# Inverses of 32x32 blocks kept beside the rest of the 64x64 matrix, one product per level, in a transformer block on one Trainium2 core

## The reference

```python
p = rmsnorm(x) @ w_in                    # RWKV-7 part, gated-DeltaNet part, two gates
y_a = (groupnorm(rwkv7_recurrence(...)) + bonus) * out_gate      # 32 heads of 64
# gated DeltaNet, 16 heads of 128, in chunks of 64 frames:
lower = jnp.where(strict, einsum(kb, k) * decay, 0.0)            # 64x64, strictly lower
tmat = triangular_solve(eye + lower, eye)                        # its unit-triangular inverse
u = tmat @ vb; wk = tmat @ (kb * exp(gc))                        # then a scan over 4 chunks
x = x + rmsnorm((sigmoid(gA) * y_a + sigmoid(gB) * y_b) @ w_out)
x = x + rmsnorm((silu(xn @ w_gate) * (xn @ w_up)) @ w_down)      # xn = rmsnorm(x)
```

## Time and profile before

| what | value |
|---|---|
| median of 3 runs | 2117.68 us (2117.16 to 2118.33) |
| profiled execution, its own time | 2115.33 us |
| its span, first to last instruction | 2113.6 us |
| TensorE busy | 2079.8 us, 98% |
| VectorE busy | 1423.1 us, 67% |
| ScalarE busy | 1095.8 us, 52% |
| GpSimd busy | 160.7 us, 8% |
| mean granted TensorE clock | 0.997 of full speed |

### The profile page before, as it was taken

How to read it: one execution, slowest core, us unless ns; L and a number is a source line. 1 busy time by engine, 2 the same in 40 slices (tenths; PEclk the granted TensorE clock), 3 DMA queues, 4 the chain that set the end, 5 groups by cost and what they waited for, 6 DMA issues and landing times.

```text
span 2113.6 us, 49505 instructions
## 1 busy us (share of the span) xinstructions
PE 2079.8 (98%) x20584; PEld 1798.8 (85%) x20584; DVE 1423.1 (67%) x2864; ACT 1095.8 (52%) x2075; POOL 160.7 (8%) x277
## 2 busy tenths in 40 slices
PE   8999999999999999999999999999999999999998
PEld 7988888889889888888988888888888888878886
DVE  6768777877877877787787784755445445454446
ACT  6655655655555565565555554554444444444444
POOL 3001011011101101101100110000000000000000
PEclk9999999999999999999999999999999999999999
DMA  9744544445444455544554434655555555544553
GB/s 248 179 124 129 148 130 127 125 125 155 126 125 128 124 142 134 133 126 125 145 133 127 116 105 133 219 193 185 190 187 190 187 182 178 196 172 186 198 186 132
DMA packets 387534, 327.31 MB, mean 155 GB/s; under 512 B 11808, under 2 KB 334352, under 8 KB 381200
## 3 DMA queue, kind: packets, MB, share of 16 engines
q1 hardware_dynamic: 375552, 319.16, 51.3%
q10 hardware_dynamic: 11792, 5.42, 1.0%
HBM read 322.45 MB, written 2.10 MB: 154 GB/s over the span
## 4 chain that ended last, share of the span: by engine, by line
PE 92%; DVE 2%; issue 1%; ACT 1%; DVEq 0%; ACTq 0%
PE ps L296 15%; PE ps L1067 13%; PE ps L298 12%; PE ps L297 12%; PE ps L594 11%; PE ps L598 11%; PE ps L596 11%; PE ps L419 1%; PE ps L421 1%; PE ps L420 1%; PE ps L1165 1%; PE ps L2239 0%; PE ps L1235 0%; PE ps L1206 0%; DVE early L1532 0%
## 5 line engine op out<-in xcount | busy, mean ns | idle before, releaser
L296 PE MATMUL ps<-hi_all,xh 128*128 128x384 f32 (+1 forms) x1568 | 561.2, 358 | 4.0 <-DVE lo_all L291 4.0
L586 DVE TENSOR_TENSOR lo_all<-stage,hi_all 128x1024 fp32r<-128x1024 f32 x263 | 322.0, 1225 | 349.1 <-ACT hi_all L582 348.7
L298 PE MATMUL ps<-hi_all,xl 128*128 128x384 f32 (+1 forms) x1568 | 528.8, 337 | 0.0
L297 PE MATMUL ps<-lo_all,xh 128*128 128x384 f32 (+1 forms) x1568 | 527.2, 336 | 0.0
L582 ACT ACTIVATE hi_all<-stage 128x1024 fp32r<-128x1024 f32 x260 | 275.4, 1060 | 398.0 <-PE ps L598 398.0
L291 DVE TENSOR_TENSOR lo_all<-stage,hi_all 128x768 fp32r<-128x768 f32 (+1 forms) x400 | 378.6, 967 | 106.3 <-ACT hi_all L286 103.1
L286 ACT ACTIVATE hi_all<-stage 128x768 fp32r<-128x768 f32 (+1 forms) x400 | 324.6, 833 | 182.3 <-PE ps L298 174.4
L296 PEld LDWEIGHTS ps<-hi_all,xh 128*128 128x128 f32 x1568 | 294.2, 188 | 36.1 <-issue 24.4
L297 PEld LDWEIGHTS ps<-lo_all,xh 128*128 128x128 f32 x1568 | 295.1, 188 | 0.7
L298 PEld LDWEIGHTS ps<-hi_all,xl 128*128 128x128 f32 x1568 | 294.6, 188 | 1.0
L594 PE MATMUL ps<-hi_all,xh 128*128 128x512 f32 x704 | 276.4, 393 | 1.8 <-DVE xl L541 1.8
(11 more groups left out here) (291 smaller groups left out, 2676.7 us busy)
## 6 DMA issues: line engine op xcount, KB each, us to landing
stage<-in_w_in SPq DMA_DIRECT2D x288, 512.0 KB, 5.6
stage<-in_ffn_w_gate SPq DMA_DIRECT2D x44, 1024.0 KB, 5.2
stage<-in_ffn_w_up SPq DMA_DIRECT2D x44, 1024.0 KB, 5.1
stage<-in_ffn_w_down SPq DMA_DIRECT2D x22, 2048.0 KB, 7.6
stage<-in_w_out SPq DMA_DIRECT2D x16, 344.0 KB, 4.3
stage<-in_w_out SPq DMA_DIRECT2D x8, 516.0 KB, 4.6
stage<-in_w_in SPq DMA_DIRECT2D x8, 448.0 KB, 5.9
stage<-in_w_out SPq DMA_DIRECT2D x8, 336.0 KB, 4.4
```

The source lines that it names most:

```text
L296: nc.tensor.matmul(o, xh[:, kc, xs], high, start=kc == 0, stop=False)
L297: nc.tensor.matmul(o, xh[:, kc, xs], low, start=False, stop=False)
L298: return nc.tensor.matmul(o, xl[:, kc, xs], high, start=False, stop=kc == KC - 1)
L586: nc.vector.tensor_tensor(wlo[b], src, whi[b].bitcast(F32), ALU.subtract).then_inc(ffn_lo, 1)
```

## The change

The diagonal blocks' inverses move into a tile `es` of 64 columns per matrix: columns 0 to 31 hold what is left of L's block (ScalarE copies it there, `ec0` to `ec3`), columns 32 to 63 the inverse so far. Each level is one batch of 24 products, `P0` to `P4`: `xs` (the transposed level mask of the left half, negated by the subtraction that follows) times the columns of `es` that can still change. `LEVEL = (0, 4, 8, 16, 48)` gives the first of them, so the batches are 32, 60, 56, 48 and 16 columns wide. VectorE subtracts the batch from `es` (`x0` to `x4`), masks the next level out of its left half (`m0_` to `m3_`) and transposes that (`a0` to `a3`); `a4` is the transpose of the finished inverse. `Y` and `X` are the old `Y4` and `X4`.

Besides: the root in `output_dve` runs its first Newton round in part 1 and the other two in part 2, so there are five parts; the turn of the previous unit stands before `Y` and after one quantum behind `P4`; the masks `lev` change their form; a tile `pad` of 32 bytes and the order of `hidT`, `hh`, `hl` before the small tiles put these and the tiles from `dd` on at multiples of 64 bytes from the start of a partition. Before, `dd` to `ym`, `hidT`, `hh` and `hl` stood 32 bytes past such a multiple.

```diff
-def rsqrt(nc, dve, done, tag, unit, y, v, t, lag=0):
+def rsqrt(nc, dve, done, tag, unit, y, v, t, lag=0, rounds=range(3)):
...
-    step(nc.vector.tensor_scalar(y.bitcast(I32), v.bitcast(I32), -0.5, 1597463007.0, ALU.mult, ALU.add))
-    step(nc.vector.tensor_scalar(v, v, -0.5, None, ALU.mult))
-    for _ in range(3):
+    if rounds[0] == 0:
+        step(nc.vector.tensor_scalar(y.bitcast(I32), v.bitcast(I32), -0.5, 1597463007.0, ALU.mult, ALU.add))
+        step(nc.vector.tensor_scalar(v, v, -0.5, None, ALU.mult))
+    for _ in rounds:
...
+            pad = tb("pad", [P, 8])
             dd = tb("dd", [P, NT, P])
...
+            es = tb("es", [P, 6, 2 * BK])
+            x64 = tb("x64", [P, 6, CH])
+            xs64 = tb("xs64", [P, 6, CH])
...
-            yc = tb("yc", [P, 6, BK // 2])
...
+            LEVEL = (0, 4, 8, 16, 48)
@@ mix_pe
-                after_y, after_x = (1, 2, 1, 0, 1), (1, 1, 1, 1, 2)
+                after_p = (1, 2, 2, 2, 1, 1, 2)
...
-                    if i < 4:
-                        for p in range(6):
-                            for k, q in enumerate(QUADS):
-                                last = mm(ps[q, 2, 16 * p:16 * p + 16], tr[q, p, 0, QUADS[k % 2]], half1(xi[q, p, :], m, 0))
...
-                            for q in QUADS:
-                                last = mm(ps[q, 2, T + 16 * p:T + 16 * p + 16], xs[q, p, :], yc[q, p, :])
...
+                    for p in range(6):
+                        for k, q in enumerate(QUADS):
+                            if i == 0:
+                                last = mm(ps[q, 2, CH * p:CH * p + BK], xs64[q, p, QUADS[k % 2]], tr[q, p, 0, QUADS[k % 2]])
+                            else:
+                                last = mm(ps[q, 2, CH * p + LEVEL[i]:CH * p + CH], xs[q, p, :], es[q, p, LEVEL[i]:])
+                    E.step(f"P{i}", last)
+                    fill(after_p[i])
+                if prev:
+                    turn_pe(pe, u, 1)
...
@@ mix_act
+                after(V, "g")
+                for k, q in enumerate(QUADS):
+                    fn(f"ec{k}", es[q, :, 0:BK], tr[q, :, 0, QUADS[k % 2]])
...
@@ output_dve
-                    rsqrt(nc, dve, VB, "r", u, rs[:], stt[:], rst[:], lag)
+                    rsqrt(nc, dve, VB, "r", u, rs[:], stt[:], rst[:], lag, range(1))
+                elif part == 2:
+                    rsqrt(nc, dve, VB, "r", u, rs[:], stt[:], rst[:], lag, range(1, 3))
                     tt("yn", y4, y4, rs[:, 0:4].unsqueeze(2).to_broadcast([P, 4, RH]))
...
@@ mix_dve
-                after_y, after_x = (2, 2, 0, 1), (2, 0, 1, 1)
+                after_p = (2, 2, 2, 2, 1)
...
+                for i in LV:
+                    after(E, f"P{i}")
+                    if i == 0:
+                        after(A, "ec3")
+                    cs = slice(LEVEL[i], BK if i == 0 else 2 * BK)
+                    tt(f"x{i}", es[:, :, cs], es[:, :, cs], ps[:, 2, 0:6 * CH].rearrange("p (a j) -> p a j", a=6)[:, :, cs],
+                       ALU.subtract)
                     done(f"x{i}")
-                    V.step(f"a{i}", nc.vector.transpose(xs[:], xi[:]))
-                    fill(after_x[i])
-                    if i < 3:
-                        output(i + 1)
+                    if i < 4:
+                        tt(f"m{i}_", xi[:], es[:, :, 0:BK], lev[:, i:i + 1, :].to_broadcast([P, 6, BK]))
+                        done(f"m{i}_")
+                        V.step(f"a{i}", nc.vector.transpose(xs[:], xi[:]))
+                    else:
+                        V.step("a4", nc.vector.transpose(xi[:], es[:, :, BK:]))
+                    fill(after_p[i])
+                    if i > 0:
+                        output(i)
...
@@ feed-forward part
+        hidT = sb("hidT", [P, FKC, T])
+        hh = [sb(f"hh{i}", [P, 2, T], F32R) for i in range(2)]
+        hl = [sb(f"hl{i}", [P, 2, T], F32R) for i in range(2)]
         ssx = sb("ssx", [P, NT])
...
-        hidT = sb("hidT", [P, FKC, T])
-        hh = [sb(f"hh{i}", [P, 2, T], F32R) for i in range(2)]
-        hl = [sb(f"hl{i}", [P, 2, T], F32R) for i in range(2)]
```

More of the change, by code:

```diff
@@ L754, in _ @@
                         chain(nc.gpsimd.memset(wide[:], 0.0))
[L755 to L758, removed]
+                        chain(nc.gpsimd.memset(v[:, :, 1, :], 1.0))
+                        keep(v[:, :, 1, :], [[-2 * m, nb], [0, m]], 0, 1)
+                        keep(v[:, :, 1, :], [[2 * m, nb], [0, m]], m - 1, -1)
+                        if i == 0:
+                            chain(nc.gpsimd.tensor_tensor(lev64[:], wide[:, 0:CH], wide[:, CH:P], ALU.add))
+                        else:
+                            fold(lev[:, i - 1, :], wide)
                     fold(eye[:], ident)
@@ L1267, in mix_pe @@
[L1267 to L1273, removed]
-                            for q in QUADS:
-                                last = mm(ps[q, 2, T + 16 * p:T + 16 * p + 16], xs[q, p, :], yc[q, p, :])
[L1276 to L1279, removed]
-                        for p in range(6):
-                            for even, odd in (QUADS[0:2], QUADS[2:4]):
-                                last = mm(ps[even, 2, T + BK * p:T + BK * p + BK], yw[odd, p, :], xs[odd, p, :])
@@ L1283, in mix_pe @@
-                    E.step(f"X{i}", last)
-                    fill(after_x[i])
-                    if i == 3 and prev:
-                        turn_pe(pe, u, 1)
+                    for p in range(6):
[4 more added lines that the diff above has]
+                                last = mm(ps[q, 2, CH * p + LEVEL[i]:CH * p + CH], xs[q, p, :], es[q, p, LEVEL[i]:])
@@ new lines, in mix_pe @@
+                    E.step(f"P{i}", last)
+                    fill(after_p[i])
+                if prev:
+                    turn_pe(pe, u, 1)
+                after(V, "a4")
+                pe.sem_inc(tiles, 1)
+                for p in range(6):
+                    for even, odd in (QUADS[0:2], QUADS[2:4]):
+                        last = mm(ps[odd, 2, BK * p:BK * p + BK], tr[even, p, 0, QUADS[1]], xi[even, p, :])
+                E.step("Y", last)
+                fill(after_p[5])
+                after(A, "yw")
@@ L1287, in mix_pe @@
+                pe.sem_inc(tiles, 1)
+                for p in range(6):
+                    for even, odd in (QUADS[0:2], QUADS[2:4]):
+                        last = mm(ps[even, 2, T + BK * p:T + BK * p + BK], yw[odd, p, :], es[odd, p, BK:])
+                E.step("X", last)
+                fill(after_p[6])
                 assert q_at[0] == FIRST + QU, q_at[0]
@@ L1760, in mix_dve @@
                 done("g")
-                for k, q in enumerate(QUADS):
-                    V.step(f"tn{k}", nc.vector.transpose(xi[q, :, :], tr[q, :, 0, QUADS[k % 2]]))
-                done("tn3")
-                tt("xm", xi[:], xi[:], lev[:, 0:1, :].to_broadcast([P, 6, BK]))
-                done("xm")
-                tt("xi", xi[:], eye[:].unsqueeze(1).to_broadcast([P, 6, BK]), xi[:], ALU.subtract)
-                done("xi")
-                V.step("xs", nc.vector.transpose(xs[:], xi[:]))
+                tt("m0", x64[:], tr[:, :, 0, :], lev64[:].unsqueeze(1).to_broadcast([P, 6, CH]))
+                done("m0")
+                V.step("xs", nc.vector.transpose(xs64[:], x64[:]))
+                tt("hs", xi[:], x64[:, :, 0:BK], x64[:, :, BK:], ALU.add)
+                done("hs")
+                tt("h", es[:, :, BK:], eye[:].unsqueeze(1).to_broadcast([P, 6, BK]), xi[:], ALU.subtract)
                 after(A, "ah1")
@@ L1816, in finish_dve @@
                         fill(LAST[c][k - 1])
-                for part_ in range(4):
+                for part_ in range(5):
                     output_dve(dve, u, 0, part_)
-                    fill(1 if part_ < 3 else 0)
+                    fill((1, 0, 1, 1, 0)[part_])
                 fill(OQ + QBUF - 2 - n_at[0])
@@ L1891, in _ @@
                 load_out_weights(sp)
-                wait(sp, V, "xi", NU - 1)
+                wait(sp, V, "h", NU - 1)
                 wait(sp, E, "g", NU - 1)
```

68 lines of the change are left out of this document (26 added, 42 removed).

## The result

The changed kernel takes 2091.84 us (median of 4 runs, 2091.00 to 2093.31), the one before 2117.42 in the same session: ratio 0.9881, 95% interval 0.9868 to 0.9893. That is 25.6 us less. The forecast was 2087, 30.4 less; rival (a), in which the address does nothing, stood at 2093.5.

The account below looks back on a forecast made before the run. TensorE, busy 98% of the span, was taken as the bound. Profiled 2115.33 us, less 28.6 (batches), plus 4.5 (turn), less 6.5 (address), gives 2084.7; the profile lay 2.35 under the median, so 2087, range 2077 to 2105.

Parts of the forecast that it names:

- rival (a): Down products: the address of the stationary operand does nothing, 6.5 us more than forecast, 2093.5 us; chance 0.18.
- The saving on the batches: TensorE's batches: 6.04 us per unit falls to 4.25, saving 1.79 us per unit, 28.6 us over 16 units.
- What the new batches cost: P0 to P4 on TensorE: 4.25 us per unit; 60 columns take 0.86 us, 0.27 more than a narrow batch.
- Rival (d): Batches on bank 2: the four 32x32 tiles do not run four at once; 44 us more, 2127 us, slower; chance 0.06.
- Does VectorE keep up?: VectorE's list up to the turn: no mask late at P1 to P4; mix ends at 1042.7, TensorE arrives at 1042.5.
- The turn's wait: TensorE waits for VectorE's mix at the turn: 0.3 us per unit, 4.5 us over 15 units; bounds nothing and 1.3.
- GpSimd's hold: GpSimd's three products at the root's end hold VectorE through the shared port: 0.6 us taken, 0.8 seen before.
- ... and the root in two pieces cost nothing: VectorE's output parts: splitting the root costs nothing, because TensorE does not wait for it.
- Tiles on multiples of 64 bytes: Down products: hh and hl on such addresses save 6.2 ns on each of 1056 products, 6.5 us.
- I cost it at nothing: ScalarE's four copies, about 1.5 us: the bank is free some tenths ahead; if not, each 0.1 us late costs 1.6.
- a sign of being wrong: Prediction wrong if wide batches exceed 1.2 us, the turn waits over 1 us, or TensorE waits at P1 to P4.
- VectorE's total: In the changed profile, VectorE's total time should be 15 to 25 us up.

Follow-up runs that it names:

- Experiment 8: The changed kernel with batches P2, P3 and P4 also 60 columns wide, the extra columns not read: 2096.25 us, ratio 0.9900 to the kernel before.
- experiment 7: The changed kernel with the norm's root in one piece again, all three rounds in part 1 ahead of x2: 2088.18 us, ratio 0.9863 to the kernel before.
- experiment 1: The kernel before with only the address change (filler tile pad; hidT, hh and hl declared earlier): 2116.54 us, against 2116.79 before.
- experiment 2: The changed kernel with the hh and hl buffers laid into tiles xh and xl: 2086.47 us, ratio 0.9857 to the kernel before.
- experiment 3: The changed kernel with one of ScalarE's two split steps put behind its copies, in the last unit only: 2086.17 us, ratio 0.9857 to the kernel before.

## Why the prediction was right and wrong

The saving on the batches, which carries the forecast, came as reckoned. The time, though, is nearer to rival (a)'s 2093.5 than to the forecast's 2087, and it is luck that it came so near: 6.5 us for the address didn't come and 5.3 in the last unit weren't foreseen, and old gaps of that unit, a shorter front and cheaper turns and batches made up for some 5 of it. By the two profiled executions the change is 23.3 us, by the medians 25.6, since the profile before lay 2.1 under its median and the one behind at it.

- **"What the new batches cost": right.** 4.20 us for 4.25; saved 6.04 - 4.20 = 1.84 a unit for 1.79, 29.4 us over 16 units for 28.6. `P1` took 0.83 us for 0.86. Experiment 8 shows that width costs on the chip what the rows say, 0.44 us a unit for the three wider batches. The sentence of the Trainium skill (TensorEngine Tiling, Instruction Overhead) by which one column costs as much as 60 doesn't hold for these fp32 products on 32x32 tiles: 0.59 us at 16 columns, 0.62 at 32, 0.71 at 48, 0.83 at 60. Up to some 32 columns there is such a floor, beyond it there is none.
- **Rival (d), tiles that don't run four at once: refuted.** 60 columns would have shown 1.1 us more than a narrow batch and show 0.24. One after another its 48 records would take 2.48 us at 0.86 ns a column (an estimate from the earlier trace rows), and they take 0.83. The Trainium skill's rule in TensorEngine Tiling, Gotcha 1: PSUM Pressure, on row tiles in one bank, is not what these four tiles on bank 2 do; each of them writes 32 partitions of its own, and tiles on the same partitions were not tried.
- **"Does VectorE keep up?": right in each start** to 0.3 us. The turn's wait, forecast at 0.3 us a unit, 4.5 in all, was 0.16 and 2.3 (experiment 7), with 0.8 more in one unit and 0.5 in the last: 3.6. GpSimd's hold was 0.2 us on the two quanta (1.95 for 1.74) and 0.24 on the mask (0.60 for 0.36) for the 0.6 taken.
- **"... and the root in two pieces cost nothing": wrong by its size.** It put GpSimd's products behind `P3`, where VectorE has no slack, instead of before it, where it had 0.41 us: it is what made the turn wait, 2.3 us over the units and 0.5 in the last.
- **"Tiles on multiples of 64 bytes": the step that failed,** 6.5 us forecast, 0 measured (experiment 1). Rival (a) held. The observation, two paces for two addresses, was sound, and experiment 2 shows the address as a cause; the property named was the wrong one. Its size was off too: 12 starts of the earlier trace rows gave 0.2267 us a product, where that stage has 0.228 to 0.229 on the mean, so even the right property is worth 5.0 us and not 6.5. With one slow and one fast address, alignment was only one of many differences between them.
- **"I cost it at nothing" (ScalarE's copies): right in 15 units, wrong in the last.** I read the cover in a unit in which quanta belong to the next unit. In the last one ScalarE's list holds it for a bank of the output projection, and the copies stand behind. Price 5.3 us (experiment 3). The prediction had named a wait at `P1` to `P4` for the transposes as a sign of being wrong, and there it stands, 3.85 us at `P1`. Against this, gaps between the batches of the kernel before in that unit (0.35, 1.24, 0.80 and 0.53 us, 2.9 in all) went away, so the unit as a whole became only 0.9 us longer.
- **The sum.** -29.4 for the batches, +3.6 for turns, 0 for the address, +5.3 for the last unit, -2.9 for its old gaps, -1.0 front and +0.5 feed-forward make -23.9; the span shows -23.3. The rest, 0.04 us a unit, I can't place. VectorE's total rose by 13.1 us, less than the 15 to 25 forecast.

## What to carry to other kernels

Read a term's cover in the first, a middle and the last pass of a loop: where the filler work changes its kind, another engine's list can hold the new instruction. Orders written out for each engine are one object: moving one piece of filler in TensorE's list alone cost 35 and 48 us here, where a gain of 7 was hoped for. A correlation with an address says that the place matters, not which property of it; test the property before it stands in a sum. And give the work that slows a neighbour (GpSimd under VectorE) to the stretch in which that neighbour has to wait anyway.

## What the runs showed of the hardware

- The place of the stationary operand's tiles changes the pace of float32r products with 512 columns: 228.6 ns against 233.3 over a stage of 1056, in otherwise equal programs (experiment 2). 64 and 128 byte multiples don't. Which property of the place counts is open.
- A gap in TensorE's work can cost more than itself: behind 3.85 us and behind 1.54 us the granted clock was 0.50 for some 3 us, that is about 1.5 us more; behind 2.45 us it cost 1.3 to 2.7 more. Behind equal gaps it fell in some units or executions and not in others.
- Four 32x32 tiles on one PSUM bank, 48 records: 0.59 us at 16 columns, 0.62 at 32, 0.71 at 48, 0.79 at 56, 0.83 at 60.
- GpSimd under VectorE holds both: where GpSimd's products of 256 elements, 1011.32 to 1014.17 us, meet VectorE's split of two quanta from 1012.48 on (experiment 7), the split takes 2.50 us instead of 1.79 and the last of the products 1.34 instead of 0.74.
